# One first norm group inside the projection loop, output products between the value units, and 28 unread products

## What is computed

```python
proj = rmsnorm(x) @ w_in                    # q, k, v, z, xbc, dt
attn = rmsnorm(attend(q, k, v), g_attn)     # block-sparse attention; samples read paged caches
y, ssm_new = ssd_scan(...)                  # Mamba-2 group
y = (y + d_skip * xs) * silu(z)
y = _rms(y.reshape(bn, l, SSM_GROUPS, SSM_WIDTH // SSM_GROUPS)) * g_ssd   # 2 groups of 512
out = concatenate([attn, y]) @ w_out
h = x + out;  h = h + peer_ffn(rmsnorm(h)); y_out = rmsnorm(h)
```

## Time and profile before

| | us |
|---|---|
| median of 3 runs | 1196.28 (1191.41 to 1199.67) |
| the profiled execution | 1196.83 |
| its span | 1194.8 |
| PE busy in the span | 1150.9 (96%) |
| DVE, ACT, POOL busy | 788.4, 568.3, 744.7 |

### The profile page before, as it was taken

One profiled execution on the slowest core, in us unless ns is written; L12 is line 12 of the kernel. 1 busy time (PEld: TensorE's weight loads), 2 busy tenths in 40 slices (PEclk: granted clock), 3 DMA queues, 4 the chain that ended last, 5 costly groups with the idle time before them and its releaser, 6 DMA issues.

```text
span 1194.8 us, 24222 instructions
## 1 busy us (share of the span) xinstructions
PE 1150.9 (96%) x7585; PEld 1012.7 (85%) x7585; DVE 788.4 (66%) x1722; ACT 568.3 (48%) x1282; POOL 744.7 (62%) x621
## 2 busy tenths in 40 slices
PE   8999999839999999999999999999999999999997
PEld 7877777509979999999999999998888888888876
DVE  6689786783179999100899999994445546666534
ACT  3323223442345555565555554444555555555545
POOL 0066350024726799889666666666767788789654
PEclk9999999857999999999999999999999999999999
DMA  7568666772644476666544554444665688778643
GB/s 251 169 214 274 204 204 202 262 260 67 188 142 142 136 201 185 186 177 194 150 141 143 143 141 143 143 140 142 193 188 189 187 303 273 237 275 290 194 157 107
DMA packets 109179, 225.13 MB, mean 188 GB/s; under 512 B 12754, under 2 KB 21570, under 8 KB 108586
## 3 DMA queue, kind: packets, MB, share of 16 engines
q1 hardware_dynamic: 105858, 212.60, 57.3%
q0 software_dynamic: 2304, 8.39, 2.0%
q10 hardware_dynamic: 936, 3.14, 0.7%
HBM read 215.80 MB, written 8.19 MB: 187 GB/s over the span
## 4 chain that ended last, share of the span: by engine, by line
PE 70%; issue 1%; DVE 0%; POOL 0%; ACT 0%; DVEq 0%; POOLq 0%; ACTq 0%
PE bank L1616 30%; PE bank L1646 30%; PE bank L1626 5%; PE bank L1569 2%; PE bank L1581 1%; PE bank L1593 1%; PE bank L1666 0%; PE bank L1683 0%; POOL hl L1509 0%; DVE acts L2042 0%; PE bank L1674 0%; ACT acts L1852 0%; POOL hl L1494 0%; PE bank L1701 0%; PE bank L1659 0%
## 5 line engine op out<-in xcount | busy, mean ns | idle before, releaser
L1494 POOL TENSOR_TENSOR hl<-ring,hl 128x512 fp32r<-128x512 f32 x448 | 586.0, 1318 | 184.6 <-ACT hl L1732 176.1
L1732 ACT CAST hl<-ring 128x512 fp32r<-128x512 f32 x512 | 317.1, 620 | 290.4 <-PE bank L1646 156.3
L1616 PE MATMUL bank<-split,hl 128*128 128x256 f32 x3072 | 378.4, 282 | 0.4 <-ACT hl L1732 0.3
L1616 PEld LDWEIGHTS bank<-split,hl 128*128 128x128 f32 x3072 | 366.2, 188 | 0.9 <-issue 0.5
L1646 PE MATMUL bank<-hl,split 128*128 128x512 f32 x1524 | 353.6, 394 | 0.0
L1646 PEld LDWEIGHTS bank<-hl,split 128*128 128x128 f32 x1524 | 286.0, 188 | 67.7 <-issue 0.9
L501 PE MATMUL pj<-xn,ring 128*128 128x264 f32 x672 | 158.4, 392 | 0.7 <-ACT proj L778 0.7
L2012 DVE TENSOR_TENSOR split<-acts,split 128x256 fp32r<-128x256 f32 x128 | 129.4, 1036 | 39.5 <-ACT split L1828 35.1
L501 PEld LDWEIGHTS pj<-xn,ring 128*128 128x128 f32 x672 | 126.2, 192 | 24.9 <-issue 4.6
L2019 DVE TENSOR_TENSOR hl<-ring,hl 128x512 fp32r<-128x512 f32 x64 | 45.2, 706 | 117.6 <-ACT hl L1732 117.6
L483 POOL TENSOR_TENSOR wo<-ring,wo 128x512 fp32r<-128x512 f32 x32 | 42.2, 1325 | 106.5 <-ACT wo L930 106.4
(11 more groups left out here) (355 smaller groups left out, 1096.3 us busy)
## 6 DMA issues: line engine op xcount, KB each, us to landing
ring<-in_uv SPq DMA_DIRECT2D x256, 256.0 KB, 2.8
ring<-in_v_rows SPq DMA_DIRECT2D x256, 256.0 KB, 3.3
ring<-in_w_ring SPq DMA_DIRECT2D x76, 512.0 KB, 4.0
room<-in_cache_k SPq DMA_DIRECT2D x64, 128.0 KB, 3.8
room<-in_cache_v SPq DMA_DIRECT2D x28, 256.0 KB, 3.3
hs<-in_state_ssm SPq DMA_DIRECT2D x8, 512.0 KB, 5.0
out_ssm_s<-hs SPq DMA_DIRECT2D x8, 512.0 KB, 6.0
acts<-x_rows SPq DMA_DIRECT2D x8, 512.0 KB
```

The lines of the kernel that those rows point to most:

```text
L1494: nc.gpsimd.tensor_tensor(hl[:, r % HL, 1], raw[:, r], hl[:, r % HL, 0].bitcast(F32), ALU.subtract).then_inc(lo_done, 1)
L1616: mm = nc.tensor.matmul(out, hl[:, r % HL, m, k * P:(k + 1) * P], split[:, x, kk, 0:TP], start=(kk == 0 and n == 0), stop=(kk == KD - 1 an ...
L1732: nc.scalar.copy(hl[:, r % HL, 0], raw[:, r]).then_inc(hi_done, 1)
```

## The change

Group 0 of the SSD norm moves ahead. ACT makes silu(z) for tiles 0 to 3 inside the loop at c = 5 (`gates(0)`) and for the rest right behind the loop (`gates(1)`); DVE multiplies with it at c = 6 (`gate(0)`) and right behind `ssd_out` of c = 7 (`gate(1)`). ACT squares group 0 at the end of c = 6 (`squares(0)`, into the free tile `sq0` and into `mix[:, 7]`), DVE adds these squares at c = 7, and PE makes their sum before `turn_probs`. Group 1 follows behind value unit 2. The factors are made group by group (`ssd_factor`, `ssd_scaled`), in `tmp`.

The attention norm on DVE goes behind `mix_low` of the SSD tiles and `values_kept(0)`. The six SSD halves of the output projection are put between the value units 5 to 7, `values(0)`, `values(1)`, `spread_rates` and `late_sums`. Three of the eight value loads (n = 3, 4, 6) move from SP to POOL, and units 2 and 6 get a new home in `xn`. Each unit has a semaphore of its own. Twenty-eight products whose result nobody reads are added: 16 ahead of the first SSD half, 8 at the end of the first program, 4 at the start of the second. ACT's order of piece casts changes with it: pieces 0 and 1 ahead of the first `mixr`, and pieces 8 to 10 behind the wait for `att_s` (before, pieces 6 to 10 stood there).

```diff
+        val_homes.append(part(xn[:].rearrange("p k n -> p (k n)"), 0, SIDE, D // 2))
+        V_HOME = (2, 3, 4, 0, 1, 2, 4, 0)
+        sq0 = part(flatp, 0, 3, NT)
+        sq1 = part(ssd, 24 * P - 4 * NT, 4, NT)
...
+                    if n == 1:
                         sp.wait_ge(ys_done, KD - 1)
                         for s in (1, 2):
                             sp.wait_ge(hs_out[s], 16 * (KD // HS))
+                    elif n == 2:
+                        sp.wait_ge(pj_copied, N_IN)
                     else:
+                        sp.wait_ge(unit_used, {0: KU - 2, 5: KU + 1, 7: KU + 4}[n])
...
+                    pool.wait_ge(unit_used, {3: KU - 1, 4: KU, 6: KU + 3}[n])
+                    for j in range(SIDE):
+                        b = q * SIDE + j
+                        at = pool.value_load(ptab[0:1, b * NPG + g:b * NPG + g + 1], min_val=0, max_val=t["n_pool"] - 1)
+                        pool.dma_start(val_homes[V_HOME[n]][:, j],
+                                       t["cache_v"][bass.ds(at, 1)].rearrange("a p n -> p (a n)")[:, m * 4 * P:(m + 1) * 4 * P]
+                                       ).then_inc(val_full[n], 16)
+                pool.wait_ge(ptab_in, 16)
+                values(3)
+                values(4)
                 for n in range(2 * N_OUT):
+                    if n == 2:
+                        values(6)
                     pool.wait_ge(o_hi, n + 1)
...
                 turn_sample_probs()
+                pe.wait_ge(pre_s, 1)
+                pe.wait_ge(own_copied, 1)
+                nc.tensor.matmul(pj[1][:, 0:NT], ones, sq0[:, 0], start=True, stop=True).then_inc(sum_s, 1)
                 turn_probs(KD - 1)
                 pe.wait_ge(h1_done, KD)
                 value_unit(0)
                 value_unit(1)
                 attend(KD - 1)
                 value_unit(2)
+                pe.wait_ge(pre_s, 2)
+                nc.tensor.matmul(pj[0][:, 0:NT], ones, sq1[:, 0], start=True, stop=True).then_inc(sum_s, 1)
                 value_unit(3)
                 pe.wait_ge(y_done, KD)
                 value_unit(4)
...
+                for n in range(16):
+                    nc.tensor.matmul(yb[:, 0:P], flat, flat, start=True, stop=True)
                 pe.wait_ge(pj_copied, N_IN)
+                pe.wait_ge(sums_read, 2)
+                out_half(N_IN, 0, 1, True, False)
+                value_unit(5)
+                pe.wait_ge(o_copied, 2 * KD)
+                pe.wait_ge(pre_p, 1)
+                nc.tensor.matmul(hd[0][:, 0:TP], ones, sq_att[:, 0, 0:TP], start=True, stop=True).then_inc(sum_p, 1)
+                out_half(N_IN + 1, 1, 1, True, False)
+                value_unit(6)
                 values(0)
+                out_half(N_IN + 2, 2, 1, True, False)
+                value_unit(7)
+                out_half(N_IN + 3, 3, 1, True, False)
+                values(1)
+                spread_rates()
+                out_half(N_IN + 4, 4, 1, True, False)
+                late_sums()
+                out_half(N_IN + 5, 5, 1, True, False)
                 pe.wait_ge(mix_lo, 6)
...
+                pe.wait_ge(res_done, 1)
+                for n in range(8):
+                    nc.tensor.matmul(pj[0][:, 0:P], flat, flat, start=True, stop=True)
```

ACT behind the loop, in its new order (the old order in the listing above from L904 on):

```diff
+                gates(1)
                 for b in range(NQ):
                     sample_exps(b)
                 exps(KD - 1)
+                squares(1)
                 probs_out(KD - 1)
+                act.wait_ge(diffs6, 2)
+                nc.scalar.activation(s6[:, 4:6], s6[:, 4:6], ACT.Exp, scale=SCALE).then_inc(rates6, 1)
                 attended(KD - 1)
+                act.wait_ge(var_s, 1)
+                nc.scalar.activation(tmp[:, 0], tmp[:, 0], ACT.Sqrt).then_inc(root_s, 1)
                 act.wait_ge(o_copied, 2 * KD)
                 act.wait_ge(ys_done, KD)
                 nc.scalar.activation(sq_att[:, :, 0:TP], mix[:, 0:KD, 0:TP], ACT.Square).then_inc(sq_p, 1)
+                act.wait_ge(var_s, 2)
+                nc.scalar.activation(tmp[:, 1], tmp[:, 1], ACT.Sqrt).then_inc(root_s, 1)
...
+                out_high(0, 2)
                 for n in range(2):
                     act.wait_ge(mixed_s, 4 * n + 4)
                     nc.scalar.copy(mixr[:, KD + 4 * n:KD + 4 * n + 4], mix[:, KD + 4 * n:KD + 4 * n + 4]).then_inc(mix_hi, 1)
+                out_high(2, 6)
+                act.wait_ge(var_p, 1)
+                nc.scalar.activation(rr[:, 0, 0:TP], rr[:, 0, 0:TP], ACT.Sqrt).then_inc(root_p, 1)
+                out_high(6, 8)
...
                 act.wait_ge(att_s, 1)
                 nc.scalar.activation(sq_att[:, :, TP:NT], mix[:, 0:KD, TP:NT], ACT.Square).then_inc(sq_l, 1)
+                out_high(8, 11)
```

More of the change, by code:

```diff
@@ L433, in _ @@
                 values(2)
-                values(3)
                 sp.wait_ge(ys_done, KD)
@@ L437, in _ @@
                     sp.dma_start(sel6[j * SPAN:j * SPAN + NH], t["sel"]).then_inc(sel6_in, 16)
-                for n in range(4, VU):
-                    values(n)
+                values(5)
+                values(7)
                 sp.wait_ge(qk_ready, 2 * KD)
@@ L689, in _ @@
                 value_unit(4)
[L690 to L700, removed]
                 def out_half(i, d, half, start, stop):
@@ L894, in _ @@
                     copy(CONV_CH + 4 * c + 3)
+                    if c == KD - 3:
+                        gates(0)
+                    if c == KD - 2:
+                        squares(0)
                 def sample_exps(b):
@@ L1221, in sample_rates @@
                     nc.vector.tensor_tensor(s6[:, 5], s6[:, 3], s6[:, 6], ALU.subtract).then_inc(diffs6, 1)
+                sample_rates()
+                normal(KD - 1)
                 def sample_factors():
@@ L1250, in _ @@
-                nc.vector.reciprocal(rr[:, 1:3], rr[:, 1:3]).then_inc(var_s, 1)
-                dve.wait_ge(sum_p, 1)
-                link(nc.vector.tensor_scalar(rr[:, 0, 0:TP], hd[0][:, 0:TP], 1.0 / D, EPS, ALU.mult, ALU.add))
-                nc.vector.reciprocal(rr[:, 0, 0:TP], rr[:, 0, 0:TP]).then_inc(var_p, 1)
-                dve.wait_ge(root_s, 1)
-                for k in range(KD):
-                    nc.vector.scalar_tensor_tensor(out=mix[:, KD + k], in0=mix[:, KD + k], scalar=par[:, P_GSSD + k:P_GSSD + k + 1],
-                                                   in1=rr[:, 1 + k * GROUPS // KD], op0=ALU.mult, op1=ALU.mult).then_inc(mixed_s, 1)
@@ L1258, in _, with ssd_factor @@
-                dve.wait_ge(root_p, 1)
-                for k in range(KD):
-                    nc.vector.scalar_tensor_tensor(out=mix[:, k, 0:TP], in0=mix[:, k, 0:TP], scalar=par[:, P_GAT + k:P_GAT + k + 1],
-                                                   in1=rr[:, 0, 0:TP], op0=ALU.mult, op1=ALU.mult).then_inc(mixed_p, 1)
+                def ssd_factor(n):
+                    dve.wait_ge(sum_s, n + 1)
+                    nc.vector.tensor_scalar(tmp[:, n], pj[1 - n][:, 0:NT], GROUPS / D, EPS, ALU.mult, ALU.add).then_inc(sums_read, 1)
+                    dve.wait_ge(sums_read, n + 1)
+                    nc.vector.reciprocal(tmp[:, n], tmp[:, n]).then_inc(var_s, 1)
@@ new lines, in ssd_scaled @@
+                def ssd_scaled(n):
+                    dve.wait_ge(root_s, n + 1)
+                    for k in range(4 * n, 4 * n + 4):
+                        nc.vector.scalar_tensor_tensor(out=mix[:, KD + k], in0=mix[:, KD + k], scalar=par[:, P_GSSD + k:P_GSSD + k + 1],
+                                                       in1=tmp[:, n], op0=ALU.mult, op1=ALU.mult).then_inc(mixed_s, 1)
+                dve.wait_ge(qk_ready, 2 * KD)
+                ssd_factor(0)
+                dve.wait_ge(sq_s, 2)
@@ L1535, in _ @@
                     opened(pe, *sc_ready)
+                    for n in range(4):
+                        nc.tensor.matmul(stb[:, 0:P], ones, ones, start=True, stop=True)
                     def square_sums():
```

112 lines of the change are left out of this document (58 added, 54 removed).

## The result

| | before | after | forecast |
|---|---|---|---|
| median of 5 runs, us | 1199.36 (1191.41 to 1200.73) | 1190.10 (1189.29 to 1190.79) | 1180.3 |
| ratio, 95% interval | | 0.9934 [0.9906, 0.9962] | 0.986 |
| profiled execution, its span | 1196.83, 1194.8 | 1190.79, 1189.1 | 1180.3, 1178.3 |
| PE busy in the span | 1150.9 | 1154.2 | |

The ratio makes about 8 us, which is within 1% of before; the five runs of before lie 9.3 us apart, and the 6.0 us between the two profiled executions are inside the interval too. The time lies in the forecast range (1173 to 1192), but at its upper end, and the likeliest case (1176 to 1184) did not come.

What follows compares the result with a forecast made beforehand. PE's idle time (23.3 us) and low clock ahead of the attention halves were taken as the bound. First half at 247.3 plus 36.2 gives 283.5 instead of 300.01: 16.5 off the 1194.8 span, plus 2.0, 1180.3 us; range 1173 to 1192.

Steps and rivals of the forecast that it cites:

- PE: unit 2 and second sum until 240.2: Chain to the first SSD half: PE ends value unit 2 and the group 1 norm sum at 240.2, without a transfer wait.
- covered, with nothing to spare: POOL's loads for units 3 and 4, at 1.6 us an issue, land at 240.3, against 241 on PE.
- Two times four scalings at 1.6: Chain to the first SSD half: DVE's eight scalings behind `ssd_factor(1)` take 1.6 us per four, ending at 245.7.
- if the chain were earlier they would be the bound: The 16 unread products ahead of the first SSD half, 5.1 us together, end with the chain at 247.3.
- `pre_p`: Behind the first SSD half: PE waits 1.2 us for DVE's `values_kept(0)` and adds, 252.6 against 251.2.
- the fifth half on ACT's pieces: Pieces 8 to 10 stand behind `att_s` on ACT, so the fifth SSD half waits 2.0 us.
- I keep one such drop, 2.3: Clock loss between first half and attention halves: one drop, at `values(1)` and `spread_rates` together, 2.3 us.
- I expect `values(0)` not to drop the clock: Between the SSD halves: `values(0)` costs no clock, as full products stand on both sides.
- The border: Twelve unread products between the two programs: cost 1.7 us, clock gain 1.7, net 0, between 1.5 better and 2 worse.
- The clock stays low: Rival: the products don't lift PE's clock; halves and units cost 14 us more, gain 2 to 3, 1194; chance 0.12.
- POOL's loads are slow: Rival: POOL's issues take longer than 1.6 us, gain gone at 3.0; chance 0.08 for over 1194, half beyond 1208.
- middle case: Rival: first half at 251 instead of 247.3, or half of the clock loss, 1184 to 1190; chance 0.2.

Runs made afterwards that it cites:

- e1: The kernel after, with all eight value loads issued by SP again in the order of the units; 1183.5 us.
- e2: The kernel after, with POOL waiting until unit 2's pages have landed before it issues its loads; 1184.5 us.
- e10: e5 with POOL's first weight subtraction held back until DVE's eight SSD scalings are done; 1178.0 us, ratio 0.9836.
- e11: e5 with 8 unread products ahead of the first SSD half; 1175.1 us, ratio 0.9832.
- e3: The kernel after without the 16 unread products ahead of the first SSD half; 1191.0 us.
- e5: e1 with units 4 and 5 loaded ahead of the sel rows, no unread products, ACT's pieces 8 to 11 ahead of the wait on att_s; 1175.5 us, ratio 0.9822.
- e6: e1 without the 16 unread products, the 12 at the border kept; 1183.0 us, ratio 0.9876.
- e7: The kernel after without any of the 28 unread products; 1188.6 us, ratio 0.9932.
- e4: The kernel after without the 12 unread products at the border of the two programs; 1188.8 us.
- e9: The kernel after, with ACT casting pieces 8 to 11 ahead of its wait for att_s; 1189.9 us.
- e12: e5 with the edits of e10 and e11 together; 1179.2 us, ratio 0.9833.
- e8: The kernel before with only the 12 unread products at the border added; ratio 0.9998.

## Why the prediction was right or wrong

**The first half: forecast 20.2, measured 28.1.** By its own steps:
- *"PE: unit 2 and second sum until 240.2", and POOL's loads "covered, with nothing to spare".* This is the step that failed. I asked when units 3 and 4 would land and never what their traffic does to unit 2, which SP loads in the same microseconds: 4.6 us. e1 and e2 show it from both sides, with 11.1 and 11.0 where 11.5 was forecast. The price of an issue itself was inside its bounds (1.15 us, bounds 0.9 to 1.7) and cheaper than the 1.6 taken, so the eight came out sooner and closer together (no run changes that alone).
- Behind that wait, unit 2 and the sum ran at the low clock (1.91 and 1.25, where e1 and e2, with no wait there, have 1.05 and 0.71): 1.5 us, a consequence of the first.
- *"Two times four scalings at 1.6".* Mis-sized by 2.0 (5.27 for 3.2). The rows of before had DVE's small operation slowed beside POOL's subtraction; the forecast used that row for the rival on transfers only, and not for the chain, where POOL's subtraction now lies at the scalings. e10 shows the cause. The Trainium skill says it ("SBUF — State Buffer", section "Who interferes with whom"): a DVE instruction with two SBUF inputs contends with a GpSimd instruction that reads SBUF. By that, the trace agrees: 5.27 beside the subtraction, 3.22 beside transfer issues.

4.6 + 1.5 + 2.0, less 0.2 at the tail, are 7.9 of the 8.0 that are missing. The reciprocal took 1.80 (forecast 1.75). The unread products were priced at 5.1 us for the sixteen, by a working that doesn't give that (128 of 264 columns of 1.07 us are 0.52 each, 8.3 together); the runs have 3.84 to 5.95, so the price was right by luck. They ended at 25.6, so that with a chain at the forecast 20.2 they would have been the bound, as "if the chain were earlier they would be the bound" says: unit 2's lateness and its cure both hand the path to them, and e1 shows it.

**From the first half to the attention halves: forecast 36.2, measured 38.5.** The work itself was right, 27.4 forecast and 27.08 in e11. The waits were over-sized, 4.2 for 6.5: `pre_p` 1.15 (1.2 forecast, and luck: DVE's adds took 4.3 us and not 2.4, and PE came later by nearly as much), unit 6 0.56 (1.8), the fifth half on ACT's pieces 1.93 (2.0), the end 0.53 (1.5). *"I keep one such drop, 2.3"* is the term that failed: the clock cost 7.2. By halves at the low clock:

| half | the term in the forecast | lengths in the runs, us |
|---|---|---|
| first, without the 16 products (e3, e5, e6, e7, e10) | | 5.06, 5.19, 5.52, 4.94, 4.89 |
| first, with them (after, e1, e2, e4, e9), with 8 (e11, e12) | full clock | 4.42, 3.14, 3.18, 3.13, 4.41; 3.14, 3.60 |
| second, behind the wait for the adds | full clock | after 3.25; 3.25 to 3.29 in eight others; 4.60, 4.78, 4.34 in e4, e9, e12, where that wait was 4.40, 3.73, 3.75 |
| third, behind `values(0)` | full clock | after 5.63; 3.14 in all eleven others that have it |
| fifth, behind `values(1)` and `spread_rates` | one drop, about 5.3 | after 4.96; 4.5 to 5.6 in nine others, 3.15 in e11 and e12 |

So the drop at the spread was forecast rightly. The first half was still partly at the low clock (1.3); the wait of 2.55 us ahead of it isn't enough to explain that, as e4 has one of 3.07 and a half of 3.13. And the third (2.5) went against *"I expect `values(0)` not to drop the clock"*, which held in every other kernel and not in the one that was to be forecast. The fifth lost 1.8, the sixth 0.4, and the small products around them the rest. Why the third fell in after alone these runs don't settle.

**The border: forecast 0 net, measured 0.1 worse** (11.84 for 11.73; e8 0.9998). Cost 1.8 for the 1.7 forecast. For the gain the reason given isn't shown: the clock held in four of the seven kernels with the products and in four of the seven without, so the net came out as forecast but may be luck.

**The loop** was right: the own products started no later.

**The signs of being wrong.** POOL's load rows stayed far under 2 us, and DVE was not slowed beside them (0.15 us for 2 columns at 229.86 in after, the scalings in e2). The third sign came: PE's rows of the halves at 5 us, 5.63 and 4.96 in after.

**The rivals.** *The clock stays low* was no all-or-nothing case; a third of it came, 4.9 beyond the one drop for its 14. *POOL's loads are slow* did not come. Its rule in the Trainium skill ("SBUF — State Buffer", section "SBUF: two separate sides"), lock-out while POOL writes descriptors, shows nowhere: 0.54 us for nearly every issue, beside busy DVE, in after and in e2. That rule speaks of two-port modes, and which of DVE's instructions here run in one, no row shows. What came in its place is on the other side of the same step: not the issue, but the transfer. Here too the Trainium skill has a sentence ("DMA: Bandwidth & Descriptors", section "Issuing engines are not separate DMA queues"), that transfers begun by any engine run on the same 16 DMA engines and interleave. e1 and e2 agree, and here it was 4.5 us of PE's time. The *middle case* had the size (1184 to 1190, measured 1190.1, at its edge) and the place wrong in part.

**What the change was worth, part by part.** The early norm, DVE's new order and the halves between the units together bring the 18.7 us of the first half (46.8 to 28.1) and, when the loads are in order, 25.5 (to 21.3 in e5); no run takes these three apart. The 28 unread products: nothing (e7). POOL as a second issuer: a loss of about 6 us (6.8 at the next norm sum from after to e1; 5.6 in the times from e7 to e6, though e6 still has the 12 at the border). By first half and waits alone e6 is 9.9 us ahead of e7, and 4.0 of that went back at the clock and the border. The piece order: about 2 us of waiting (e9), not to be told in the time alone.

## What to carry to other kernels

A second engine that issues transfers gave no second way into memory here: before work is moved to it, list which earlier transfer is still under way and who waits for it, and issue in the order of need. Whoever moves a chain earlier must look at what every other engine does beside it in its new place; here the same eight operations on DVE were 60% longer. And unread products that lift a clock should be costed like any work on the path: here the sixteen paid themselves back and no more, and for the twelve at the border no gain is shown. Last, where the clock costs several us more or less from kernel to kernel and no edit is shown to be why, judge an edit by the wait that it removes, and repeat the runs before a small gain is believed.

## What the runs showed of the hardware

- A plain 256 KB page load issued by POOL holds it for 0.54 us, one per 1.15 us with the page's number read ahead of it, and its twelve loads landed in 5.5 to 10.4 us (median 7.1). SP's twenty landed in 2.7 to 12.3 (median 4.5), against 3.3 before.
- DVE instructions with two inputs in SBUF and POOL's subtraction slow each other: eight scalings 3.2 to 5.3, two low parts 2.5 to 3.5, the two large adds 1.9 (before) to 6.4 (e9); POOL 1.25 to 1.84 each in e10. Which of the two pays changes: at the adds DVE took 2.91 and POOL's four 6.78 in after, DVE 5.82 and POOL's four 4.97 in e4. POOL's transfer issues did neither.
- The clock at the border: two tiles took 7.3 to 7.4 us in four kernels with the unread products ahead of them (after, e2, e3, e8) and in four without (e4, e5, e7, e10); 8.2 to 9.05 in three with them (e1, e6, e9) and in three without (before, e11, e12). Each is one execution. With four of seven either way, no run shows that the products hold the clock there.
